# Rotated halves of rotary and axial positions: transfers within SBUF in place of products with a constant matrix

## The reference, cut to what matters

```python
def apply_rope(x, cos, sin):
    ...
    x1, x2 = jnp.split(x, 2, axis=-1)
    return jnp.concatenate([x1 * c - x2 * s, x2 * c + x1 * s], axis=-1)

def apply_axial_rope(x, cos, sin):
    ...
    out = jnp.concatenate([xr1 * cr - xr2 * sr, xr1 * sr + xr2 * cr,
                           xc1 * cc - xc2 * sc, xc1 * sc + xc2 * cc], axis=-1)
```

## Time and profile before

| what | us |
|---|---|
| median of 3 runs | 3100.09 (3083.01 to 3108.54) |
| the profiled execution | 3093.86 |
| its span | 3092.1 |
| TensorE busy | 2951.1 |
| VectorE busy | 1952.1 |
| ScalarE busy | 1273.1 |
| GpSimd busy | 217.2 |

### The profile page before, as it was taken

The page is one execution under the profiler, slowest core; times in us unless marked ns, Lnnn a source line. Parts: engine busy times, 40 slices in busy tenths (PEclk is TensorE's granted clock), DMA queues, the critical chain, the costliest instruction groups (busy, mean ns, idle before and its releaser), DMA issues.

```text
span 3092.1 us, 56026 instructions
## 1 busy us (share of the span) xinstructions
PE 2951.1 (95%) x23406; PEld 2792.2 (90%) x23406; DVE 1952.1 (63%) x3163; ACT 1273.1 (41%) x2209; POOL 217.2 (7%) x311
## 2 busy tenths in 40 slices
PE   8899999999998999999988999999999998999899
PEld 7788889977897999999976789999999998887899
DVE  5655688565577867767476456666566655435655
ACT  4454554444555454222444334223522234235443
POOL 1210000022000000000010020000000001000000
PEclk8999999999999999999999999999999999999999
DMA  5435467533445754555231214444354443242454
GB/s 195 126 106 161 137 206 244 181 108 103 144 161 184 240 197 164 174 166 162 88 116 42 68 48 157 164 160 148 99 175 162 160 136 116 96 143 88 132 195 140
DMA packets 245473, 447.71 MB, mean 145 GB/s; under 512 B 14483, under 2 KB 87076, under 8 KB 244452
## 3 DMA queue, kind: packets, MB, share of 16 engines
q1 hardware_dynamic: 239584, 430.79, 42.3%
q10 hardware_dynamic: 5636, 13.33, 1.3%
HBM read 443.01 MB, written 1.05 MB: 144 GB/s over the span
## 4 chain that ended last, share of the span: by engine, by line
PE 64%; DVE 6%; ACT 4%; issue 2%; POOL 1%; DMA 0%; ACTq 0%; DVEq 0%; POOLq 0%
PE ps L1296 51%; DVE split L2058 1%; PE ps L1373 1%; ACT split L1748 1%; PE ps L1374 1%; PE ps L1375 1%; PE ps L1251 1%; DVE A L2360 1%; PE ps L1326 1%; PE ps L1330 1%; DVE A L2055 1%; PE ps L1327 1%; PE ps L1587 1%; PE ps L1201 1%; PE ps L1350 1%
## 5 line engine op out<-in xcount | busy, mean ns | idle before, releaser
L1296 PE MATMUL ps<-AR,split 128*128 128x256 f32 x18576 | 2222.5, 280 | 31.5 <-DVE A L2249 6.4
L1296 PEld LDWEIGHTS ps<-AR,split 128*128 128x128 f32 x18576 | 2168.4, 189 | 76.2 <-issue 33.8
L2058 DVE TENSOR_TENSOR split<-raw,split 128x1024 fp32r<-128x1024 f32 (+2 forms) x728 | 809.5, 1149 | 603.3 <-ACT split L1748 595.3
L1748 ACT ACTIVATE split<-raw 128x1024 fp32r<-128x1024 f32 (+2 forms) x728 | 686.3, 987 | 786.8 <-PE ps L1296 683.3
L2331 DVE SCALAR_TENSOR_TENSOR junk<-A,cb 128x1024 bf16<-128x1024 f32 x144 | 175.7, 1220 | 38.9 <-DMA A<-w_modT 36.8
L2058 DVE TENSOR_TENSOR AR<-A,AR 128x256 fp32r<-128x256 f32 (+2 forms) x292 | 144.8, 496 | 57.4 <-ACT A L1795 34.4
L2331 DVE SCALAR_TENSOR_TENSOR A<-A,cb 128x1024 f32<-128x1024 f32 x144 | 175.4, 1218 | 0.0
L2572 POOL TENSOR_TENSOR A<-A 128x256 f32<-128x256 f32 x57 | 42.1, 739 | 1651.2 <-ACT A L1764 1642.3
L1817 ACT ACTIVATE AR<-A 128x256 fp32r<-128x256 f32 (+1 forms) x132 | 68.4, 526 | 193.9 <-DVE A L2181 193.9
L2055 DVE SCALAR_TENSOR_TENSOR A<-A,ps 128x256 f32<-128x256 f32 (+1 forms) x196 | 95.2, 506 | 60.8 <-ACT A L1813 47.4
L1813 ACT ACTIVATE A<-ps 128x256 f32<-128x256 f32 (+1 forms) x132 | 63.0, 490 | 130.2 <-PE ps L1296 129.2
(11 more groups left out here) (247 smaller groups left out, 2530.1 us busy)
## 6 DMA issues: line engine op xcount, KB each, us to landing
A<-w_modT SPq DMA_DIRECT2D x144, 512.0 KB, 4.2
raw<-w_in SPq DMA_DIRECT2D x120, 512.0 KB, 4.0
raw<-w_gu SPq DMA_DIRECT2D x80, 512.0 KB, 5.1
raw<-ffn_a_in SPq DMA_DIRECT2D x80, 512.0 KB, 4.5
raw<-ffn_b_in SPq DMA_DIRECT2D x80, 512.0 KB, 4.4
raw<-ret_in SPq DMA_DIRECT2D x48, 512.0 KB, 4.3
raw<-w_down SPq DMA_DIRECT2D x44, 512.0 KB, 4.8
raw<-ffn_a_out SPq DMA_DIRECT2D x44, 512.0 KB, 4.4
```

Of the source, the lines that this page charges most:

```text
L1296: mm = e.matmul(out[:, s:s + NT], wt[:, c, m_], xs(k0 + c, a + s, a + s + NT), start=first and part + s == 0, stop=last and part == 2 and ...
L1748: e.activation(hi, self.raw_view(q), ACT.Copy).then_inc(*self.mark(("w hi", q)))
L2058: return self.e.tensor_tensor(out, v, hi.bitcast(F32), ALU.subtract)
```

## The change

The matrices `rot32` and `rot64` are gone from the constants, and their signs go into the sine tables. In place of the product, SyncE begins transfers from the raw buffer to the target in SBUF, half by half with the partitions exchanged: four of 32 partitions for a rotary tile, two of 64 for an axial one. It waits for ScalarE's copy first. The copy frees the bank of PSUM. The raw buffer comes free when the transfers have landed and the cosine step has read it. VectorE multiplies the target by the sines in place, after the landing; the cosine product goes to the temporary; the sum is as before.

```diff
--- before.py
+++ after.py
@@ -47,28 +47,24 @@
     f32 = np.float32
     out = {}
     eye = np.eye(128, dtype=f32)
-    rot32 = np.zeros((128, 128), f32)
-    rot64 = np.zeros((128, 128), f32)
-    for m in range(128):
-        b, d = m // 64 * 64, m % 64
-        rot32[b + (d + 32) % 64, m] = -1.0 if d < 32 else 1.0
-        rot64[(m + 64) % 128, m] = -1.0 if m < 64 else 1.0
+    lead32 = np.where(np.arange(128) % 64 < 32, -1.0, 1.0)[:, None]
+    lead64 = np.where(np.arange(128) < 64, -1.0, 1.0)[:, None]
     heads = np.zeros((128, 128), f32)
     heads[:64, :64] = 1.0 / 64
     heads[64:, 64:] = 1.0 / 64
-    out["base"] = np.concatenate([eye, rot32, rot64, heads], axis=1)
+    out["base"] = np.concatenate([eye, heads], axis=1)
     pos = np.arange(NT, dtype=f32)
     inv = (f32(10000.0) ** (-np.arange(0, 64, 2, dtype=f32) / f32(64))).astype(f32)
     ang = (pos[:, None] * inv[None, :]).astype(f32).astype(np.float64)
     pick = np.arange(128) % 32
-    out["rope"] = np.concatenate([np.cos(ang).T[pick], np.sin(ang).T[pick]], axis=1).astype(f32)
+    out["rope"] = np.concatenate([np.cos(ang).T[pick], np.sin(ang).T[pick] * lead32], axis=1).astype(f32)
     inv = (f32(10000.0) ** (-np.arange(64, dtype=f32) / f32(64))).astype(f32)
     t = np.arange(NT)
     pick = np.arange(128) % 64
     parts = []
     for q in ((t // 64).astype(f32), (t % 64).astype(f32)):
         ang = (q[:, None] * inv[None, :]).astype(f32).astype(np.float64)
-        parts += [np.cos(ang).T[pick], np.sin(ang).T[pick]]
+        parts += [np.cos(ang).T[pick], np.sin(ang).T[pick] * lead64]
     out["axial"] = np.concatenate(parts, axis=1).astype(f32)
 
     def tiled(a):
@@ -1447,17 +1443,6 @@
                 n += P
         mm.then_inc(*self.mark(("full", f)))
 
-    def rotary(self, f, dst, rawb, tmpb, scale):
-        k, o = rawb.get()
-        raw = self.A[:, o:o + NT]
-
-        def turned():
-            tmpb.get()
-            self.e.wait_ge(*self.after(("raw", f)))
-            self.e.matmul(self.bank(f)[:, 0:NT], self.base[:, 128:256], raw, start=True, stop=True).then_inc(*self.mark(("turned", f), ("raw turned", rawb.name, k)))
-
-        self.late.append(turned)
-
     def index_score(self, l, t, hd, q, k, sc, tmp):
         e, f = self.e, ("logit", l, t, hd)
         out = self.fresh(f, (4, 5))[:, 0:P * (t + 1)]
@@ -1546,7 +1531,7 @@
         def rest():
             rsb.get()
             self.e.wait_ge(*self.after(("head square", f)))
-            self.e.matmul(self.bank(f)[:, :], self.base[:, 384:512], sq, start=True, stop=True).then_inc(*self.mark(("head sum", f), sqb.freed(k)))
+            self.e.matmul(self.bank(f)[:, :], self.base[:, 128:256], sq, start=True, stop=True).then_inc(*self.mark(("head sum", f), sqb.freed(k)))
 
         self.late.append(rest)
 
@@ -1609,17 +1594,6 @@
                     o = YS[s][k * 2 + n] + m * P
                     mm = self.e.matmul(out, A[:, o:o + P], A[:, DFT + (2 + k) * 512 + n * 256:DFT + (2 + k) * 512 + (n + 1) * 256], start=k + n == 0, stop=k + n == 2)
             mm.then_inc(*self.mark(("full", f)))
-
-    def axial(self, f, dst, m, rawb, tmpb, scale=1.0, ctx=None):
-        k, o = rawb.get()
-        raw = self.A[:, o:o + NT]
-
-        def rest():
-            tmpb.get()
-            self.e.wait_ge(*self.after(("raw", f)))
-            self.e.matmul(self.bank(f)[:, 0:NT], self.base[:, 256:384], raw, start=True, stop=True).then_inc(*self.mark(("turned", f), ("raw turned", rawb.name, k)))
-
-        self.late.append(rest)
 
     def ret_scores(self, hd, ats, atb):
         e, A, KR, QR = self.e, self.A, 10240, 8192
@@ -1835,8 +1809,7 @@
         if k >= rawb.n:
             e.wait_ge(*self.after(("raw turned", rawb.name, k - rawb.n)))
             e.wait_ge(*self.after(rawb.earlier(k)))
-        e.activation(self.A[:, o:o + NT], self.bank(f)[:, 0:NT], ACT.Copy, scale=scale).then_inc(*self.mark(("raw", f)))
-        self.late.append(lambda: tmpb.get())
+        e.activation(self.A[:, o:o + NT], self.bank(f)[:, 0:NT], ACT.Copy, scale=scale).then_inc(*self.mark(("raw", f), ("free", f)))
 
     def index_twice(self, l, k0):
         i = self.asked - 1
@@ -2203,11 +2175,8 @@
         rawb.get()
 
         def turned():
-            k, o = tmpb.get()
             e.wait_ge(*self.after(("turned", f)))
-            if tmpb.earlier(k):
-                e.wait_ge(*self.after(tmpb.earlier(k)))
-            e.tensor_tensor(self.A[:, o:o + NT], self.bank(f)[:, 0:NT], self.A[:, ROPE + NT:ROPE + 2 * NT], ALU.mult).then_inc(*self.mark(("free", f), ("sine", f)))
+            e.tensor_tensor(dst, dst, self.A[:, ROPE + NT:ROPE + 2 * NT], ALU.mult).then_inc(*self.mark(("sine", f)))
 
         self.late.append(turned)
 
@@ -2460,9 +2429,7 @@
             at = 22528 + (m % 2) * 512 + 256
             e.wait_ge(*self.after("axial"))
             e.wait_ge(*self.after(("turned", f)))
-            if tmpb.earlier(k):
-                e.wait_ge(*self.after(tmpb.earlier(k)))
-            e.tensor_tensor(tmp, self.bank(f)[:, 0:NT], self.A[:, at:at + NT], ALU.mult).then_inc(*self.mark(("free", f)))
+            e.tensor_tensor(dst, dst, self.A[:, at:at + NT], ALU.mult).then_inc(*self.mark())
             e.wait_ge(*self.own())
             e.wait_ge(*self.after(("cosine", f)))
             e.tensor_tensor(dst, dst, tmp, ALU.add).then_inc(*self.mark(("rotated", f), tmpb.freed(k)))
@@ -2593,7 +2560,9 @@
             e = self.e
             j, ot = tmpb.get()
             e.wait_ge(*self.after(("raw", f)))
-            e.tensor_tensor(dst, raw, self.A[:, ROPE:ROPE + NT], ALU.mult).then_inc(*self.mark(rawb.freed(k)))
+            if tmpb.earlier(j):
+                e.wait_ge(*self.own())
+            e.tensor_tensor(self.A[:, ot:ot + NT], raw, self.A[:, ROPE:ROPE + NT], ALU.mult).then_inc(*self.mark(rawb.freed(k)))
             e.wait_ge(*self.own())
             e.wait_ge(*self.after(("sine", f)))
             e.tensor_tensor(dst, dst, self.A[:, ot:ot + NT], ALU.add).then_inc(*self.mark(("rotated", f), tmpb.freed(j)))
@@ -2629,11 +2598,13 @@
         raw = self.A[:, o:o + NT]
 
         def rest():
-            tmpb.get()
+            j, ot = tmpb.get()
             at = 22528 + (m % 2) * 512
             self.e.wait_ge(*self.after("axial"))
             self.e.wait_ge(*self.after(("raw", f)))
-            self.e.tensor_tensor(dst, raw, self.A[:, at:at + NT], ALU.mult).then_inc(*self.mark(("cosine", f), rawb.freed(k)))
+            if tmpb.earlier(j):
+                self.e.wait_ge(*self.after(tmpb.earlier(j)))
+            self.e.tensor_tensor(self.A[:, ot:ot + NT], raw, self.A[:, at:at + NT], ALU.mult).then_inc(*self.mark(("cosine", f), rawb.freed(k)))
 
         self.late.append(rest)
 
@@ -2692,6 +2663,22 @@
         self.e.dma_start(self.raw_view(q).rearrange("p (c n) -> p c n", c=nc), src[k0 * P:(k0 + nc) * P, n0:n0 + n].rearrange("(c p) n -> p c n", p=P)).then_inc(
             *self.mark(("load", q), on=f"w{q % RAW}", by=16))
 
+    def exchange(self, f, dst, rawb, half):
+
+        k, o = rawb.get()
+        raw = self.A[:, o:o + NT]
+        self.e.wait_ge(*self.after(("raw", f)))
+        for p in range(0, P, half):
+            at = p ^ half
+            done = [("turned", f), ("raw turned", rawb.name, k)] if p + half == P else []
+            self.e.dma_start(dst[p:p + half, :], raw[at:at + half, :]).then_inc(*self.mark(*done, on=f"t{k % 4}", by=16))
+
+    def rotary(self, f, dst, rawb, tmpb, scale):
+        self.exchange(f, dst, rawb, 32)
+
+    def axial(self, f, dst, m, rawb, tmpb, scale=1.0, ctx=None):
+        self.exchange(f, dst, rawb, 64)
+
     def mod_open(self, where, q):
         self.e.wait_ge(*self.after(self.mod_ready))
         self.load_mod(where, q)
@@ -2724,14 +2711,14 @@
         mem["cb"] = sb("cb", 2048)
         mem["junk"] = sb("junk", 1024, dt=BF16)
         mem["split"] = [sb(f"split{i}", 2 * 4 * 512, dt=F32R) for i in range(SPLIT)]
-        for name, n in (("base", 512), ("ones", 128), ("cols", NCOLS), ("small", 256), ("epsc", 1), ("fil", 2048), ("mods", 288), ("gsc", 48), ("lgs", 80)):
+        for name, n in (("base", 256), ("ones", 128), ("cols", NCOLS), ("small", 256), ("epsc", 1), ("fil", 2048), ("mods", 288), ("gsc", 48), ("lgs", 80)):
             mem[name] = sb(name, n)
         with nc.sbuf_tensor("A", [P, ARENA], F32) as A:
             mem["A"] = A
         mem["AR"] = sb("AR", ARENA, dt=F32R)
         ps = mem["ps"] = es.enter_context(nc.psum_tensor("ps", [P, 4096], F32))
         banks = [ps[:, i * 512:(i + 1) * 512] for i in range(8)] + [ps[:, i * NT:(i + 1) * NT] for i in range(8)]
-        sems = {n: es.enter_context(nc.semaphore("s_" + n)) for n in SEMS + LOADS + tuple(f"w{i}" for i in range(RAW)) + tuple(f"m{i}" for i in range(MODS))}
+        sems = {n: es.enter_context(nc.semaphore("s_" + n)) for n in SEMS + LOADS + tuple(f"w{i}" for i in range(RAW)) + tuple(f"m{i}" for i in range(MODS)) + tuple(f"t{i}" for i in range(4))}
 
         K = Counts()
```

## The result

| kernel | median us | lowest to highest | runs |
|---|---|---|---|
| before | 3095.74 | 3083.01 to 3108.54 | 4 |
| after | 3135.34 | 3133.12 to 3142.87 | 4 |

The ratio is 1.0093, 95% interval 1.0055 to 1.0131: the changed kernel is slower by 29 us of 3100 (17 to 41). The forecast was 3094, 3074 to 3126.

The account below looks back on a forecast made before the run. TensorE, busy 95% of the span, was taken as the bound. Products -13 us and waits on VectorE +7 gave -6 from the profiled 3093.9, so 3088; runs' median lies 6.2 higher, hence 3094 us, range 3074 to 3126.

Parts of the forecast that it names:

- 54 x 0.24 = 13.0 us: TensorE: each removed rotation product frees the distance from its start to the next start, 13.0 us in all.
- 3.4 us off: TensorE beside attention: arriving earlier, it waits longer for the attention chain, 1.7 us a layer, taken off the gain.
- the 3.5 us that were to go at the two axial groups: TensorE's axial waits: 1.8 us saved at the first group, 1.7 in front of the second.
- Issue 0.37 us at the upper end, landing 2.0.: SyncE's transfers: 0.37 us an issue at most (0.09 at least), landing 2.0; rotary exchange complete 3.5 us after the copy.
- 24 hold VectorE for 41 us in all: VectorE's sine steps: of 54 tiles 30 are covered, 24 make it wait 41 us, 15.5 of them axial.
- Per layer 3.4 us, twice: 7 us.: VectorE stalls that reach TensorE: branch c's fifth tile 2.0 us, branch b's first 1.0, indexer 0.4, in each layer.
- The indexer was put at 0.4 us a layer: Indexer: its third tile, which the index scores wait for, lands late and passes 0.4 us to TensorE.
- The axial stalls: VectorE at axial tiles, 4.2 us at the first: only splits and norm's context half held; 0 taken, up to 4.
- no split waited longer for a load: Loads behind exchanges: some issued 5 to 10 us later, but with slack of two blocks and more; taken as nothing.
- A: Rival: every exchange is hidden, through cheap issues and a 1.8 us landing; 3087 or 3083 us, chance 0.15.
- C: Rival: the change does nothing, as TensorE waits the products out in front of the attention chain; 3100 us, chance 0.07.
- Rival B: Slower: late landings hold VectorE's in-order work; 3146 us at a 5 us landing, deciding from about 3.5; chance 0.13.

Follow-up runs that it names:

- the doubled kernel: The kernel before with each of its 54 rotation products done twice into the same bank: ratio 1.0028 (1.0 to 1.0057).
- the transfers unread: All 184 transfers of the changed kernel go to spare SBUF, VectorE multiplying the unturned copy; against the kernel before 1.0001 (0.9966 to 1.0037).
- rotary alone: Rotary tiles by transfers, axial tiles by products as in the kernel before; ratio to that kernel 1.0093 (1.0064 to 1.0123).
- the halved transfers: The changed kernel with each transfer cut into two of half the rows, 368 for 184; ratio to the kernel before 1.0245 (1.0202 to 1.0288).

## Why the prediction was wrong, step by step

*"... the distance from the start of the first to the start of what follows: 91.90 to 92.14, 0.24 us ... 54 x 0.24 = 13.0 us."* Mis-sized, and too low: 0.43 us, 23.2 in all by the starts in the trace, 0.40 by the stretches of the doubled kernel; the timed medians leave it open (above). A row that said so was already there: six matmuls of three axial products in 1.56 us.

*"Not all of it arrives ... 3.4 us off."* Mis-sized. Without products and transfers TensorE waits 6.5 us more than before, for the attention chain above all (L1458 19.1 us for 16.3). Of the 3.5 us that were to go at the two axial groups beside the products, TensorE's waits for VectorE to empty a bank did go (1.5 us before, none now); the rest of the 1.8 at the first group was the products' own time, counted too low. The 1.7 in front of the second group didn't go: with the transfers unread there are still 4.8 us for ScalarE's copies, 4.0 before. The copy is late by itself.

*Issue 0.37 us at the upper end, landing 2.0.* The issue is 0.59, above the upper end; the landing was nearly right, 1.9 us with no load under way and 2.7 behind one. The upper end rested on one row, loads of 128 rows, and I took fewer rows to cost the same or less. A rotary exchange was complete 4.1 us after its start (median of 38; 3.7 to 5.7), not 3.5; at the fifth tile it was 4.9 (184.16 to 189.04), since its first issue alone took 1.46. That an exchange lands no sooner than the load ahead of it was right: of the 36 begun while an earlier load was under way, none was complete before that load had landed, though single parts were (187.45 at the fifth tile, the load 188.35).

*"... 24 hold VectorE for 41 us in all ..."* 27 waits, 76.0 us. The list of places was right (fifth tile of branch c, first axial tiles, indexer), the lengths were too short: an exchange of four parts took 0.6 us more than reckoned as a rule and 1.4 at the fifth tile.

*"Per layer 3.4 us, twice: 7 us."* This is the step that failed by most. With the products gone in both, TensorE waits 24 us more when VectorE waits for the landing than when nobody does (163.6 against 139.2 us). Of those, the axial group is 5 us (9.7 against 4.8), and the rest, 19 us, is rotary: nearly three times the 7. I let one tile a stretch pass its lateness on and took the others as covered by VectorE's idle time of the stretch; but the chain of a softmax goes through VectorE two or three times a unit, and a tile that holds it there can be seen. The indexer was put at 0.4 us a layer; it was 2.5 and 4.5, since GpSimd's sum of the third tile is what the index scores wait for, and three tiles in a row queue at SyncE.

*"The axial stalls ... hold only splits and the context half of the norm: 0 taken, up to 4 as the upper end."* Failed, with 5 us: the context half of the norm is what ScalarE must do ahead of its next copies. I followed who stands behind the wait on VectorE, but not who, on ScalarE, waits for those.

*The clock.* Not a term at all. By the account it is of the size of the waits: 59 us more at the lower level, which cost up to 29 us. The clock fell in the stretches in which TensorE now stands idle, and in every kernel with more waits than before the time at the lower level is longer, mostly the more the longer the waits (rotary alone has less than its waits would have it). In the stretches with exchanges it is 34 us before, 55 without products and exchanges (and 55 with the transfers unread), 82 in the changed kernel. So some 20 of the 48 us more came with the removal of the products, before anyone waited for an exchange, and the rest with the waits. That the idle time causes it was not tried by itself.

*Right:* no split waited longer for a load to matter (ScalarE's waits for `raw` blocks 13.6 us after, 11.5 before); GpSimd's steps cost nothing by themselves; ScalarE's wait for a raw buffer exists in the indexer alone (5.7 us in 2 times) and cost nothing where nobody read the transfers. The two rivals that ended faster or level (A, C) had no support. Rival B had the right sign and the right mechanism (VectorE in order, held by an exchange) but the wrong condition: it wanted a landing of 3.5 us or more of one transfer. The landing was 2.3, and what made the exchanges late was the issues, SyncE's wait at a load ahead of them and, at the first axial tiles, the landing of that load. Nor did the four parts follow one another in full, as B would have had it: they landed 0.6 us apart in the median, as they were issued. The Trainium skill, "DMA: Bandwidth & Descriptors", section "Rules for kernel authors", says that transfers under 64 KB pay mostly overhead; the halved transfers agree, with 0.59 us an issue at either size; so does the landing with no load under way, 1.8 us for 16 KB and 2.0 for 64.

## What to carry to other kernels

Price a small transfer by its issues, not by its bytes: an exchange in four parts is four issues, and every one stands between producer and consumer. Ask too which load was issued just ahead of it. When an engine on a softmax chain is made to wait, don't net the wait against the engine's idle time of the stretch; follow each releaser two engines further, to what stands in *their* order behind it, and leave room for more time at the lower clock. And read a matmul's cost from the matmuls behind it too, since a start in the trace can come ahead of the work. When kernels differ by under 1%, compare the stretches that hold the edit, cut at the same matmuls.

## What the runs showed of the hardware

- An issue of a transfer within SBUF: 0.59 us on SyncE, 0.61 on ScalarE, 0.50 on GpSimd (medians), on SyncE for 16 KB as for 32 KB; a load of 512 KB 0.37 on SyncE.
- Landing of such a transfer with no earlier load under way: 1.8 us for 16 KB, 1.9 for 32 KB, 2.0 for 64 KB. Behind a load that had not landed: 2.7 (median), up to 5.9. No exchange of the changed kernel was complete before a load issued ahead of it (0 of 36).
- A matmul of 256 columns on plain float32 operands is two records, 0.22 us apart, and holds TensorE for 0.43 us by the starts; on rounded operands one record, 0.12 us.
- The same matmuls, far from any edit, took 26 us more in one execution than in another within 740 us, 0.118 us apart in place of 0.113. A difference of 10 or 20 us between whole kernels can't be read from one trace each.
